# Sigmoid built from the exponential, normalising and query loads in another order, router logits in column quarters

## The reference, cut to what matters

```
s = q.k / 8 + bias, masked to +-128 tokens; 8 query heads, 2 key heads, one sink logit per head
p = softmax([s, sink])[:-1];  o = p @ v
y = concat(ya, o, yc) @ w_out + b_out
x1 = layer_norm(ALPHA*x + (1+g1)*y) * gain + shift
h2 = x1 * (1+sc2) + sh2
scores = sigmoid(h2 @ router_w)              # 32 experts in 4 groups of 8
sel = scores + router_bias
best group by the sum of its two largest sel; in it the two largest: expert, gates = scores, normalised
out = layer_norm(ALPHA*x1 + (1+g2) * moe(h2, expert, gates))
```

## Time and profile before

| | |
|---|---|
| median of 3 runs | 1877.63 us (1876.48 to 1879.01) |
| profiled execution | 1878.63 us, its span 1876.8 us |
| PE busy | 1659.4 us, 88% of the span |
| DVE busy | 1317.1 us, 70% |
| ACT busy | 962.6 us, 51% |
| POOL busy | 310.8 us, 17% |
| mean DMA rate | 220 GB/s |

### The profile page before, as it was taken

One profiled execution on the slowest core, in us unless ns is written; L12 is line 12 of the kernel. 1 busy time (PEld: TensorE's weight loads), 2 busy tenths in 40 slices (PEclk: granted clock), 3 DMA queues, 4 the chain that ended last, 5 costly groups with the idle time before them and its releaser, 6 DMA issues. The chain is left out here.

```text
span 1876.8 us, 28284 instructions
## 1 busy us (share of the span) xinstructions
PE 1659.4 (88%) x8080; PEld 1315.9 (70%) x8081; DVE 1317.1 (70%) x1985; ACT 962.6 (51%) x1508; POOL 310.8 (17%) x312
## 2 busy tenths in 40 slices
PE   3999879985799999996489999999999999999950
PEld 2767558864567677775368888888888888888840
DVE  5578768985457777776376978777656956765938
ACT  2213372225577777761264866655535735544727
POOL 0000100000100101111221243223122221211223
PEclk9999899996799999997589999999999999999985
DMA  7657755226533322333567898899696796775657
GB/s 298 233 183 266 236 207 177 87 79 241 200 112 114 103 100 91 106 109 149 230 262 267 299 393 307 308 324 336 189 324 224 262 363 218 259 280 172 211 151 319
DMA packets 116323, 412.30 MB, mean 220 GB/s; under 512 B 11761, under 2 KB 47857, under 8 KB 87588
## 3 DMA queue, kind: packets, MB, share of 16 engines
q1 hardware_dynamic: 95508, 342.08, 48.0%
q0 software_dynamic: 19744, 68.20, 14.3%
q10 hardware_dynamic: 1008, 1.22, 0.2%
HBM read 332.76 MB, written 80.81 MB: 220 GB/s over the span
## 5 line engine op out<-in xcount | busy, mean ns | idle before, releaser
L1995 ACT CAST gate_up_hi<-gate_up_raw 128x1024 fp32r (+1 forms) x256 | 265.8, 1053 | 91.2 <-PE psum_up L1936 64.9
L2138 DVE TENSOR_TENSOR gate_up_lo<-gate_up_raw,gate_up_hi 128x1024 fp32r<-128x1024 f32 x256 | 300.3, 1220 | 11.7 <-ACT gate_up_hi L1995 1.1
L489 PE MATMUL proj_bank<-x_hi,w_hi 128*128 128x512 f32 x448 | 182.6, 408 | 22.7 <-DVE w_lo L601 16.3
L491 PE MATMUL proj_bank<-x_hi,w_lo 128*128 128x512 f32 x448 | 177.8, 397 | 0.0
L490 PE MATMUL proj_bank<-x_lo,w_hi 128*128 128x512 f32 x448 | 177.8, 397 | 0.0
L1931 PE MATMUL psum_gate<-gate_up_hi,x_hi 128*128 128x512 f32 x392 | 159.0, 406 | 11.9 <-DVE x_lo L2138 7.7
L1945 PE MATMUL psum_y<-down_hi,h_hi 128*128 128x512 f32 x392 | 158.0, 403 | 4.7 <-DVE h_lo L2138 4.7
L2138 DVE TENSOR_TENSOR down_lo<-down_raw,down_hi 128x1024 fp32r<-128x1024 f32 x128 | 150.9, 1221 | 8.4 <-ACT down_hi L2003 5.3
L667 DVE SCALAR_TENSOR_TENSOR conv<-y_win,cw,conv 128x1008 f32<-128x1008 f32 (+1 forms) x120 | 154.0, 1283 | 3.0
L1936 PE MATMUL psum_up<-gate_up_hi,x_lo 128*128 128x512 f32 x392 | 154.2, 393 | 0.0
L1934 PE MATMUL psum_up<-gate_up_lo,x_hi 128*128 128x512 f32 x392 | 154.1, 393 | 0.0
(11 more groups left out here) (290 smaller groups left out, 3412.6 us busy)
## 6 DMA issues: line engine op xcount, KB each, us to landing
gate_up_raw<-in_w_gate_up SPq DMA_DIRECT2D x128, 1024.0 KB
down_raw<-in_w_down SPq DMA_DIRECT2D x64, 1024.0 KB
x_raw<-in_ada_w SPq DMA_DIRECT2D x16, 1024.0 KB, 4.8
w_raw<-in_w_in SPq DMA_DIRECT2D x28, 512.0 KB, 5.6
x_raw<-in_xT SPq DMA_DIRECT2D x16, 512.0 KB, 9.9
q_kept<-q_stage SPq DMA_DIRECT2D x32, 256.0 KB, 2.8
q_tile<-q_kept SPq DMA_DIRECT2D x16, 512.0 KB, 4.2
wo<-w_out_kept SPq DMA_DIRECT2D x8, 1024.0 KB, 13.0
```

The source lines that it names most:

```text
L489: mm(bank[:, :], w_hi[side][:, k, :], x_hi[m][:, k, :], start=(k == 0), stop=False)
L491: last = mm(bank[:, :], w_lo[side][:, k, :], x_hi[m][:, k, :], start=False, stop=(k == DC - 1))
L1995: nc.scalar.copy(gu_hi[:, k, :], raw_chunk(slot, k)).then_inc(gu_high_ready, 1)
L2138: return tt(out, raw, high.bitcast(F32), ALU.subtract)
```

## The change

Sigmoid is now built as 1 / (1 + exp(-x)): ACT writes exp(-x) (`Exp`, scale -1), and the router on DVE gets two new units at its start, an add of 1 and a reciprocal over both tiles of the pair. The eight normalisations are split: pairs 0 and 1 come right after the copies of h2T, pairs 2 and 3 after the copy of O. The logits are computed with the router's weights stationary: eight matmuls of 32 columns of weights and 128 moving tokens, chunk k into the 32 partitions of quarter k mod 4 of `M[:, 2P:3P]`; ACT copies these 128x128 partial sums to SBUF, and one matmul with the constant `fold` (ones where partition mod 32 equals the column) sums the quarters and transposes into `M[:, 0:E]`. The third chunk of O is moved between quarters and fold. On SP, `load_q(2)` moves to behind the fourth output-weight load, and `load_out(1)` to ahead of the rows of gains. PE's wait for the low part of O moves from the first to the second quarter of the output projection.

```diff
@@ -68,7 +68,8 @@
 _at = 0
 for _name, _n in (("identity", P), ("ones", P), ("mean_c", P), ("earlier", P), ("expert_tie", E * EPG),
                   ("group_tie", GROUPS * GROUPS), ("e_plus_1", E), ("e_from_32", E), ("tile_starts", TILES - 1),
-                  ("minus_half", 1), ("masked", 1), ("alternating", E), ("eps", 1), ("token_tiles", TILES)):
+                  ("minus_half", 1), ("masked", 1), ("alternating", E), ("eps", 1), ("token_tiles", TILES),
+                  ("fold", E)):
     CONST[_name] = (_at, _at + _n)
     _at += _n
 CONST_W = _at
@@ -98,6 +99,7 @@
     put("masked", NEG)
     put("alternating", (-1.0) ** np.arange(E))
     put("eps", LN_EPS)
+    put("fold", p[:, None] % E == np.arange(E)[None, :])
     put("token_tiles", p[:, None] + P * np.arange(TILES)[None, :])
 
 
@@ -1078,6 +1080,7 @@
         pT = sb("pT", [P, KV_HEADS, 3, QPAIRS, P])
         r, xn, h2, x1 = (sb(n, [P, D]) for n in ("r", "xn", "h2", "x1"))
         h2T = sb("h2T", [P, DC, P])
+        logit_parts = sb("logit_parts", [P, P])
         s_max, neg_max = sb("s_max", [P, B_HEADS]), sb("neg_max", [P, B_HEADS])
         sink_arg, sink_exp = sb("sink_arg", [P, B_HEADS]), sb("sink_exp", [P, B_HEADS])
         p_sum, p_inv = sb("p_sum", [P, B_HEADS]), sb("p_inv", [P, B_HEADS])
@@ -1122,6 +1125,7 @@
             sem("xn_ready"), sem("h2_ready"), sem("x1_ready"))
         h2T_filled, h2T_ready, logits_filled, sc_ready = (
             sem("h2T_filled"), sem("h2T_ready"), sem("logits_filled"), sem("sc_ready"))
+        parts_filled, parts_ready = sem("logit_parts_filled"), sem("logit_parts_ready")
         x1_steps, x1_stored, h2_stored = sem("x1_steps"), sem("x1_stored"), sem("h2_stored")
         router_steps, router_ready, pos_filled, pos_read, pos_steps, addr_ready = (
             sem("router_steps"), sem("router_ready"), sem("pos_filled"), sem("pos_read"), sem("pos_steps"),
@@ -1180,15 +1184,17 @@
                 if k == 3:
                     sp.dma_start(rw[:, :, :], io["rw"]).then_inc(router_landed, 16)
                     sp.dma_start(rb[:, :], io["rb"]).then_inc(router_landed, 16)
+                    load_q(2)
+            load_out(1)
             sp.dma_start(x1_gain[:, :], io["ln_mix_g"]).then_inc(rows_landed, 16)
             sp.dma_start(x1_shift[:, :], io["ln_mix_b"]).then_inc(rows_landed, 16)
             sp.dma_start(h2_gain[:, :], io["mods"][2:3, :].to_broadcast([P, D])).then_inc(rows_landed, 16)
             sp.dma_start(h2_shift[:, :], io["mods"][1:2, :].to_broadcast([P, D])).then_inc(rows_landed, 16)
 
             for s in range(STEPS):
-                if s >= 1 and tile_at(s, -1) is not None:
+                if s >= 2 and tile_at(s, -1) is not None:
                     load_q(s + 1)
-                if (t := tile_at(s, 1)) is not None and t > 0:
+                if (t := tile_at(s, 1)) is not None and t > 1:
                     load_out(t)
                 if (t := tile_at(s, 3)) is not None:
                     sp.wait_ge(h2_ready, t + 1)
@@ -1246,8 +1252,9 @@
                 return yac[:, t % 2, k - QPAIRS, hl, :]
 
             def project(t, i):
+                if i == 1:
+                    pe.wait_ge(yb_low, t + 1)
                 if i == 0:
-                    pe.wait_ge(yb_low, t + 1)
                     pe.wait_ge(yac_landed[t % 2], 32 * (t // 2 + 1))
                     if t == 0:
                         pe.wait_ge(bias_landed, 32)
@@ -1269,17 +1276,19 @@
                         if k == DC - 1:
                             last.then_inc(wo_filled, 1)
 
-            def weigh(t):
-                pe.wait_ge(pT_ready, 2 * QPAIRS * (t + 1))
-                if t > 0:
-                    pe.wait_ge(yb_low, t)
+            def weigh(t, chunks):
                 n = len(blocks_of_tile(t))
-                for c, b in enumerate(blocks_of_tile(t)):
+                if 0 in chunks:
+                    pe.wait_ge(pT_ready, 2 * QPAIRS * (t + 1))
+                    if t > 0:
+                        pe.wait_ge(yb_low, t)
+                for c, b in list(enumerate(blocks_of_tile(t)))[chunks.start:chunks.stop]:
                     for g in range(KV_HEADS):
                         rows = slice(HD * g, HD * g + HD)
                         last = mm(O[rows, :], v_all[:, b, rows],
                                   pT[:, g, c, :, :].rearrange("p a b -> p (a b)"), start=(c == 0), stop=(c == n - 1))
-                last.then_inc(o_filled, 1)
+                if chunks.stop >= n:
+                    last.then_inc(o_filled, 1)
 
             def transpose_h2(t):
                 pe.wait_ge(h2_ready, t + 1)
@@ -1292,7 +1301,7 @@
                         last = tr(T[part][:, i * P:(i + 1) * P], h2[:, k * P:(k + 1) * P], ident)
                     last.then_inc(h2T_filled, 1)
 
-            def logits(t):
+            def logit_quarters(t):
                 pe.wait_ge(h2T_ready, 2 * t + 2)
                 if t == 0:
                     pe.wait_ge(router_landed, 32)
@@ -1301,8 +1310,13 @@
                     if t >= 4:
                         pe.wait_ge(pos_read, (t - 4) // 2 + 1)
                 for k in range(DC):
-                    last = mm(M[:, 0:E], h2T[:, k, :], rw[:, k, :], start=(k == 0), stop=(k == DC - 1))
-                last.then_inc(logits_filled, 1)
+                    quarter = slice(E * (k % 4), E * (k % 4 + 1))
+                    last = mm(M[quarter, 2 * P:3 * P], rw[:, k, :], h2T[:, k, :], start=(k < 4), stop=(k >= 4))
+                last.then_inc(parts_filled, 1)
+
+            def fold_logits(t):
+                pe.wait_ge(parts_ready, t + 1)
+                mm(M[:, 0:E], logit_parts[:, :], C["fold"], start=True, stop=True).then_inc(logits_filled, 1)
 
             def positions(u):
                 pe.wait_ge(router_ready, u + 1)
@@ -1328,11 +1342,15 @@
                 if route_of is not None:
                     transpose_h2(route_of)
                 if attn is not None:
-                    weigh(attn)
+                    weigh(attn, range(0, 2))
                 if (u := pair_at(s, 6)) is not None:
                     positions(u)
                 if route_of is not None:
-                    logits(route_of)
+                    logit_quarters(route_of)
+                if attn is not None and len(blocks_of_tile(attn)) > 2:
+                    weigh(attn, range(2, 3))
+                if route_of is not None:
+                    fold_logits(route_of)
 
         @block.vector
         def _(dve):
@@ -1471,6 +1489,10 @@
                 if u > 0:
                     dve.wait_ge(route_kept, u)
                     dve.wait_ge(carry_ready, u)
+                ts(sc[:, u % 2, :, :], sc[:, u % 2, :, :], 1.0, None, ALU.add).then_inc(router_steps, n.one())
+                yield after()
+                nc.vector.reciprocal(sc[:, u % 2, :, :], sc[:, u % 2, :, :]).then_inc(router_steps, n.one())
+                yield after()
                 tt(sel[:, :, :], sc[:, u % 2, :, :], rb[:, :].unsqueeze(1).to_broadcast([P, 2, E]), ALU.add
                    ).then_inc(router_steps, n.one())
                 yield after()
@@ -1616,10 +1638,10 @@
                     af(probs[:, h, 0:n], probs[:, h, 0:n], ACT.Exp, bias=neg_max[:, h:h + 1], scale=HD ** -0.5,
                        accum_out=p_sum[:, h:h + 1]).then_inc(exp_ready, 1)
 
-            def normalise(t):
+            def normalise(t, pairs):
                 n = P * len(blocks_of_tile(t))
                 act.wait_ge(p_inv_ready, t + 1)
-                for i in range(QPAIRS):
+                for i in pairs:
                     for g in range(KV_HEADS):
                         h = QPAIRS * g + i
                         af(probs[:, h, 0:n], probs[:, h, 0:n], ACT.Copy, scale=p_inv[:, h:h + 1]
@@ -1640,9 +1662,16 @@
                     for part in range(2):
                         act.wait_ge(h2T_filled, 2 * route_of + part + 1)
                         if route_of > 0:
-                            act.wait_ge(logits_filled, route_of)
+                            act.wait_ge(parts_filled, route_of)
                         nc.scalar.copy(h2T[:, 4 * part:4 * part + 4, :], T[part][:, :].rearrange(
                             "p (a b) -> p a b", a=4)).then_inc(h2T_ready, 1)
+                if z is not None:
+                    normalise(z, range(0, 2))
+                if route_of is not None:
+                    act.wait_ge(parts_filled, route_of + 1)
+                    if route_of > 0:
+                        act.wait_ge(logits_filled, route_of)
+                    nc.scalar.copy(logit_parts[:, :], M[:, 2 * P:3 * P]).then_inc(parts_ready, 1)
                 if attn is not None:
                     act.wait_ge(o_filled, attn + 1)
                     if attn >= 2:
@@ -1650,7 +1679,7 @@
                     nc.scalar.copy(yb[:, attn % 2, :, 0, :], O[:, :].rearrange("p (a b) -> p a b", a=QPAIRS)
                                    ).then_inc(yb_high, 1)
                 if z is not None:
```

(5 more changed lines are left out.)

## The result

| | before | after |
|---|---|---|
| median | 1877.66 us (1876.48 to 1879.01) | 1844.62 us (1843.98 to 1845.10, 4 runs) |
| profiled execution, span | 1878.63, 1876.8 us | 1843.98, 1842.2 us |
| PE, DVE, ACT busy | 1659.4, 1317.1, 962.6 us | 1638.7, 1323.3, 932.0 us |

The ratio is 0.9824 (0.9807 to 0.9841): 33.0 us faster by the medians, 34.6 by the profiled executions, where 28.0 was forecast. The time lies inside the forecast range.

The account below looks back on a forecast made before the run. PE was taken to bound the attention stage from 526 to 828 us, its main wait being ACT's late copy of probabilities; 5.5 + 13.4 + 9.2 + 1.4 + 1.2 - 2.7 = 28.0 us gained, forecast 1849.6 us, range 1838 to 1864.

Parts of the forecast that it names:

- start to step 3 (query load, step 2): Step 2: the earlier query load and normalising ahead of O shorten PE's waits; 9.2 us gained, ends 5.9 and 9.9.
- step 3: PE's 1.70 us idle goes, but its second scores then wait for DVE; 1.4 us gained, 0 to 3.1.
- PE's idle time, H3 to H15: Between the h2 transposes of steps 3 and 15; PE's waits for ACT's probability copy, 13.4 us listed, all go.
- logits, 12 steps: Logits in column quarters save PE 0.39 us a step, 5.5 us over 14 steps; ends +14.7 and -7.4.
- granted clock, H3 to H15: Some 3 us lost to clock dips between the h2 transposes of steps 3 and 15; 1.2 regained, -3 to 3.
- tail: Step 16 and the routing end: uncovered fold and longer routers on DVE's serial chain; net -2.7 us, 0 to -5.
- (d): Logits: quarters overlap four-fold, 0.53 us for sixteen records; 1843 us, or 1840 with all clock dips gone; chance 0.06.
- (a): Attention steps: the next wait takes over; if 1 us is missing in 12 steps, 1861.6 us; chance 0.20.
- (b): Logits: quarters don't overlap as the halves do, 5.5 becomes -7.4, 1862.5 us; chance 0.10.
- (c): Attention steps: the clock falls oftener as PE alternates quarters, fold and transposes; 13.8 us lost, 1863.4; chance 0.07.
- (e): Slower: the fold's PE, ACT, PE round trip waits for late p_inv each step; at 2.5 us, 1887; chance 0.04.
- (f): The attention and routing stage shortens, but the tail or next stage gives it all back: 1877 us; chance 0.03.

Follow-up runs that it names:

- old-logits trial: The changed kernel with the old logits put back (O whole, h2T stationary, no parts copy, no fold): 1855.83 us, ratio to before 0.9880.
- Sigmoid trial: The changed kernel with Sigmoid back on ACT and the router's add and reciprocal gone: 1860.16 us, ratio to before 0.9907.

## Why the prediction was right, and where its sum was not

The terms as forecast, and as the profiled executions have them, in us gained:

| term | forecast | measured |
|---|---|---|
| start to step 3 (query load, step 2) | 9.2 | 9.5 |
| step 3 | 1.4 | -0.3 |
| PE's idle time, H3 to H15 | 11.9 of 13.4 | 11.9 |
| logits, 12 steps | 4.7 of 5.5 | 9.5 |
| granted clock, H3 to H15 | 1.2 | 3.05 |
| what the waits cost beyond their brackets, H3 to H15 | not in the sum | 2.05 |
| rest of the stage (tail -2.7, two steps of logits 0.8, idle 1.5) | -0.4 | 0.1 |
| expert stage | 0 | -1.2 |
| sum | 28.0 | 34.6 |

*Right: what bounds, and the idle time.* From H3 to H15 all of PE's waiting goes, with 0.2 us to spare in the step shown, half of the 0.4 forecast. Which part removes it has no single answer. Putting Sigmoid or the whole normalisation back costs 15.5 and 29.8 us, putting them in alone gives 12.2 and 18.1, and together 20.2. The four parts, each taken out alone, sum to 15.5 + 29.8 + 11.2 + 7.3 = 63.8 for a gain of 33. One order of building that does add up is Exp 12.9, halves 6.7, quarters 6.1, loads 7.3 (the medians 1877.7, 1864.8, 1858.0, 1851.9 and 1844.6; Exp's 12.2 above is against the runs of before beside it). In another order the quarters would have come first, and cost 20.

*Right: the query load.* 13.21 became 4.84 us (forecast 4.99), and the wait at the start of step 2 fell from 1.70 to 0.84 (forecast: 1.03 less); 9.5 in all with 0.3 from steps 0 and 1. The trial without it gives 7.3 by medians, since there step 3 keeps its clock.

*Wrong in size: the quarters.* The step that failed was "I take 0.99, the row with the same moving length". Sixteen records take 0.57 us, close to the 0.53 worked out from the neighbouring quarter row and set aside. The earlier trace rows had both, and I took the row in halves because its moving length matched. A record with 128 moving takes 0.117 us in one column group, 0.062 in two (that row in halves) and 0.036 in four: what decides is how many groups run side by side, so the row in quarters was the one to scale. The rest of that term held: fold 0.24 (0.23), two more switches of layout at most 0.15 in the rows of O (0.20). That makes 1.81 - 0.57 - 0.24 - 0.15 = 0.85 a step against 0.39. Against the kernels with the old logits, at full clock, steps are 0.84 shorter without positions (22.50) and 0.71 with them (23.75); the forecast had said 23.2 and 24.3. Rival (d) had the mechanism, at 0.06, and its time: 1844.6 is nearer to its 1843 than to the 1849.6 forecast. The rule in "TensorEngine Tiling (Array Packing)", Key Properties, of the Trainium skill, that a change of tiling mode drains the engine, costs here no more than those 0.15 us.

*Wrong in size: the clock.* The prediction read the loss rightly, some 3 us; it is 3.05, in two steps. All of it came back, since the clock stayed full from H3 to H15, and I took 1.2 for want of a cause. So what lay beyond those 1.2 was not foreseen but luck. What makes the clock fall is still open. It fell in steps in which PE did not idle (the old-logits trial, 0.88) and stayed full in the Sigmoid trial, where PE waited 1.0 us and more in each step. Nor is it the old logits, the rival named in that trial: with them the two kernels built on the one before with the halves ran the stretch at 1.00, and the one with the new query loads at 0.98. Of the nine traces in which PE never waits from H3 to H15 one has a fall (the old logits), of the five in which it waits four have (all but Sigmoid): a hint that fewer waits mean fewer falls, and with one trace of each kernel no more.

*Missing: what a wait costs beyond its bracket.* The sum took the waits at the length shown. Each of 1.50 us cost 1.70, and 2.05 us more came back with them.

*Wrong: step 3.* The swap of one wait (1.70) for another (1.93 on DVE) was foreseen, the clock behind the second was not: from the waiting scores to H3 it is 13.85 us (503.41 to 517.26) where it was 12.27 (514.08 to 526.35), so the 1.4 turned into -0.3. Taking that wait away gave 2.8 us. The clock does not fall behind every such wait: with the old query loads the same wait of 1.91 us had no fall behind it.

*Rivals.* (a), (b) and (c) did not occur in this kernel. (e), put at 0.04, did not occur as written: neither here nor with the quarters alone does PE idle ahead of the fold, but for 0.4 us in each of the steps 16 to 18, the last with logits. A slower kernel is real all the same, and it is what the quarters make without the other parts, +20.2 us. I had its price in p_inv; it came from O's copy and what stands behind it. (f) took back 1.2 us at most, within what the expert stage varies by itself. Moving PE's wait for the low part of O, forecast at nothing, was not tried alone; with the halves alone, where it stands in its old place, PE idles nowhere from H3 to H15.

## What to carry to other kernels

When several edits attack one wait, measure them on both ends, alone and taken out: here one part is worth +11.2 us as the last one in and -20.2 as the first. Ahead of an edit that moves work of the bounding engine behind a helper's copy, list what stands behind that copy on the helper, and shorten it first. For packed matmuls scale from the row with the same number of column groups, not from the one with the same length. A short wait of the bounding engine costs more than its bracket shows, here 0.2 us at full clock, and 1.6 more where the clock fell behind it.

## What the runs showed of the hardware

- Four column quarters of 128 moving elements (sixteen f32 records) take 0.57 us, the same in one quarter 1.87. The table loads took 1.28 us each, and nothing followed them: in the kernel before, ACT's load starts at 788.46 and its sigmoid at 789.76.
- A DVE reciprocal of 128x64 took 553 ns, of 128x8 203: 6.3 ns per element.
- The granted clock fell in steps in which PE did not idle (27.56 us at 0.88, 25.99 at 0.93), and stayed at 1.00 in others in which it waited 1.05 or 1.50 us.
- A step with a wait of PE shown as 1.50 us is 1.70 us longer than one without (25.05 and 23.35), both at a clock of 1.00.
